# A decoder step on one core: the front of the first token group put in another order

## The chip, the cores and the metric

One core of a Trainium2 chip runs the whole program in one launch. The metric is the device time of that execution in microseconds (us), the median of several runs. Everything is computed in f32.

## What is computed

One layer of a decoder for 1024 prompt tokens and 8 x 4 sample tokens with the same weights, model width 1024:

```
n    = RMSNorm(x)
proj = n @ w_in            -> q | k | v | u, v_c (gelu) | mem q | gate logits
A    = chunk gating:  u * (tril(W_s) RMSNorm(v_c) + b), 128-token chunks
B    = sliding-window attention, 8 q heads / 2 kv heads, sinks, ALiBi
C    = cross-attention of 4 heads into 256 memory rows,
       k_m, v_m = RMSNorm(mem) @ w_mem_kv
h    = x + (sum_j sigmoid(gate_j) * (branch_j @ W_j)) @ w_out
y    = h + PEER(RMSNorm(h)): 8 heads, top 16 of 128^2 experts per head;
       per token 128 rows of peer_u, gelu of their dots, 128 rows of peer_v
out  = RMSNorm(y); caches of k, v, mem k, mem v are outputs too
```

## The kernel before

**Tiles and groups.** Tokens lie in nine tiles of 128 (the last one is the 32 sample tokens). Tiles form four groups, (0), (1, 2), (3, 4, 5), (6, 7, 8). Everything up to the expert queries is the *front* of a group. The expert part runs in *batches*: a batch gathers 4 rows of `peer_u` and 4 of `peer_v` for each of 128 tokens (0.5 MB a DMA, by index, issued by GpSimd), 32 batches to a prompt tile. Group 0's front has no batches beside it; the front of group g+1 is spread over the batches of group g.

**The order.** `front_units(g)` (L115) writes a group's front as a list of units. `build_steps` (L334) puts group 0's list, up to the experts of its first quarter of heads, ahead of all batches, and spreads the other lists with `spread_out`, by the costs of `costs` (L190) and the dependences of `waits_a_step` (L206). Each of the engines TensorE (`pe`, L900), ScalarE (`act`, L1252), VectorE (`dve`, L1480) and the DMA queue SyncE (`sp`, L709) walks the same list and does its own part of every unit, strictly in that order; semaphores tie the parts together. So a unit's place sets its place in four queues. GpSimd (L1867) has a list of its own: two selects that make the chunk matrices triangular, then all gathers.

**Units of group 0's front**, with their lines: `load_x`, `load_mem` (SP, L734 and L745); `square` (ScalarE, L1258: Square with the row's mean as its accumulator, then Sqrt) and `scale` (VectorE, L1501: the inverse root with one Newton step by `inverse_root`, L1486, then the row is scaled in place), argument 0 for x, 1 and 2 for the memory rows; `turn` (TensorE transposes through the identity, L907, L914; VectorE copies them into `xnT` times the norm's weight, L1508, L1515); `chunk` (L941, L948; ScalarE Gelu and mean square, L1290); `chunk_norm` (VectorE, L1518; for tile 0 it first waits for all constants of `second_in` and makes small tables); `block` (L917, L930: one 128-column block of the input projection; the four `u` blocks here, the eight q and memory-q blocks and k later); `spatial` (L951, L959; L1532; TensorE waits for GpSimd's two selects by `made`); `mem_k`, `mem_v`, `mem_turn` (L962 to L987); `values`; `scores` (L989; VectorE adds the bias and takes maxima, L1554, `m_ready`); `exps` (ScalarE, L1311); `divide` (L1585); `probs` (transposes, L1015); `mix` (L1032); `gate` (L1149: eight chunks of a gate block into one PSUM bank, four of the branch's projection into another; ScalarE Tanh, L1390; VectorE product and sum, L1662); `out` (L1173, L1679); `square_h`, `norm_h`, `turn_h` (L1400, L1689, L1183); `query` (L1193); `keys` and the top-k units.

**Gates.** There are 24 of a group, `("gate", g, i, j)` for 8 column blocks i and 3 branches j; `gate_order(0)` is (1, 0, 2). The first one in order needs only the chunk branch's features (`u_ready`), which are there before the softmax. VectorE's part of the first waits until the memory branch's mix is done, because `merged`, `sig` and `prod` share the buffer `area` with the scores: `sc` at 0 to 2047, `scT` at 2048 to 4095; `merged` at 0, `sig` at 3072, `prod` at 3840. Tile 0 uses only the second half of each head's keys in `sc` and `scT`.

**PSUM.** Each unit's results go to the next of six banks in turn (`SPOT`, `TURN`, L417); a writer waits for the reader of the bank's last user (`free`, `gone`).

**Weights.** They are streamed by SP into six slots of 2 MB (`LOADS`, L440; the rings of the gathers serve as four of them in group 0). A load is issued when the unit in `FREED` has read its slot. At the start SP issues x, the constants `FIRST`, weight 0 (`vc`), the ten constants `SECOND` and the attention bias, the two memory tiles, `load_hb(0)` (x again, for the residual) and the next five weights (L866 to L883).

**Tables.** ScalarE's functions need the right table; a load stands as ACT_TABLE_LOAD in the trace. Sqrt, Gelu and Exp/Tanh sit in different ones.

Of the kernel before, what the change touches and what calls it, by code (L numbers as in the profile page):

```python
# [14 lines left out]
DC = D // P  # L15
# [99 lines left out]
def front_units(g):  # L115
    tiles = GROUP_TILES[g]
    prompt = [t for t in tiles if t < PTILES]
    out = [("load_x", t) for t in tiles] + [("load_mem", m) for m in range(MT)] + [("square", 0), ("scale", 0)] if g == 0 else []
    out += [("turn", feed(t)) for t in tiles]
    out += [("chunk", t) for t in tiles] + [("chunk_norm", t) for t in tiles]  # L120
    if g == 0:
        out += [("square", 1), ("square", 2), ("scale", 1), ("scale", 2)]
    out += [("block", g, WK + 1 + n) for n in range(CG)]
    out += [("spatial", t) for t in tiles]
    if g == 0:
        out += [("turn", 1), ("turn", 2)]
        out += [("mem_k", m) for m in range(MT)] + [("mem_v", m) for m in range(MT)] + [("mem_turn", m) for m in range(MT)]
    out += [("block", g, n) for n in range(FU)]
    out += [("block", g, WK)]
    for n, t in enumerate(prompt):  # L130
        if n == 0:
            out += [("values", x) for x in tiles]
        out += [("scores", t)]
        out += [("exps", t), ("divide", t)]
        if n:
            out += [("mix", prompt[n - 1])]
        out += [("probs", t)]
    out += [("mix", prompt[-1]), ("keep_k", g)]
    if PTILES in tiles:
        out += [("smp_load", 0), ("knat", 0), ("smp_scores", 0)] + [("smp_mem", b) for b in range(0, 3)]  # L140
        out += [("smp_turn", 0)] + [("smp_mem", b) for b in range(3, 6)]
        out += [("smp_soft", 0)] + [("smp_mem", b) for b in range(6, B)]
        out += [("smp_probs", 0), ("smp_mem_turn", 0), ("smp_mem_soft", 0), ("smp_mix", 0), ("smp_mem_probs", 0)]
        out += [("smp_mem_mix", b) for b in range(B)]
        out += [("smp_mem_out", 0)]
    out += [("gate", g, i, j) for i in range(DC) for j in gate_order(i)]
    out += [("load_hb", t) for t in tiles if g or not starts_group(t)]
    out += [("out", t, half) for half in range(2) for t in tiles]
    out += [("square_h", t) for t in tiles]
    out += [("norm_h", t) for t in tiles]  # L150
    out += [("turn_h", t) for t in tiles]
    if PTILES in tiles:
        out += [("pack_root", 0)]
    out += [("query", g, n) for n in range(2 * PH)]
    return out
# [373 lines left out]
def build(nc, t):  # L529

    ctx = ExitStack()
    with ctx:
# [110 lines left out]
        def left(*name):  # L643
# [29 lines left out]
        y_stored = [sem(f"y_stored{n}") for n in range(2)]  # L673
        mem_stored, vc_stored, stored = sem("mem_stored"), sem("vc_stored"), sem("stored")

        FIRST = dict(ident=ident, norm1_col=norm1_col)
        SECOND = dict(chunk_g=chunk_g, ws_T=ws_T, ws_T_smp=ws_T_smp[0:SAMPLE], chunk_b=chunk_b, mem_norm_col=mem_norm_col,
                      gate_b=gate_b, sinks=sinks, idents=idents, iota16=iota16, smp_sinks=smp_sinks)
        CONSTS = dict(subT=subT, norm2_g=norm2_g, final_g=final_g)
        PACKED = 16 * (GROUPS - 1 + 2 * GROUPS)  # L680
# [29 lines left out]
        def _(sp):  # L710
# [155 lines left out]
            for n, units in STEPS:  # L866
                if n is not None:
                    expert(n)
                for u in units:
                    if u[0] in DO:  # L870
                        DO[u[0]](*u[1:])
                    if u == ("load_mem", 1):
                        load_hb(0)
                    if u == ("load_x", 0):
                        for name, a in FIRST.items():
                            send(a, t[name], first_in)
                        load_w(0)
                        for name, a in SECOND.items():
                            send(a, t[name], second_in)
                        send(bias[:, :], t["swa_bias"][:, 0, :], second_in)  # L880
                    if u == ("load_mem", 1):
                        for n_w in range(1, SLOTS_W):
                            load_w(n_w)  # L883
                    if u == ("mix", 0):
                        for name, a in CONSTS.items():
                            send(a, t[name], consts_in)
                    if u in FREED and w_next(FREED[u]) is not None:
# [365 lines left out]
        def _(act):  # L1253
# [3 lines left out]

            def square(n):  # L1258
                R = rows_of(n)
                act.wait_ge(x_in[XBUF[n]], 16 * x_before(n)[1])  # L1260
                A.settle()
                A.add(fn(n_dump[0:R, :], x_buf[0:R, XBUF[n], :], ACT.Square, scale=D ** -0.5, accum_out=mean_x[0:R, n:n + 1]))
                A.settle()
                A.add(fn(root_x[0:R, n:n + 1], mean_x[0:R, n:n + 1], ACT.Sqrt, bias=eps[0:R, :]), x_squared, n + 1)
# [134 lines left out]

            def square_h(x):  # L1400
                R, k = width(x), local(x) // P
                act.wait_ge(*gone("out", x, 1))
                act.wait_ge(*gone("out", x, 0))
                A.settle()
# [76 lines left out]
        def _(dve):  # L1481
# [179 lines left out]

            def gate(g, i, j):  # L1662
                k, W = NBR * i + j, tokens(g)
                if i == 0 and j == gate_order(i)[0]:
                    V.settle()
                    dve.wait_ge(f_mm, upto("mmix", max(x for x in GROUP_TILES[g] if x < PTILES)))
                dve.wait_ge(*gone("gate", g, i, j))
# [200 lines left out]
        def _(pool):  # L1868
            g = nc.gpsimd

            pool.wait_ge(second_in, 16 * (len(SECOND) + 1))
            g.affine_select(out=ws_T[:, :, :], in_=ws_T[:, :, :], compare_op=ALU.is_ge, fill=0.0, base=0,
                            pattern=[[0, CG], [1, P]], channel_multiplier=-1).then_inc(made, 1)
# [151 lines left out]
```

## Time and profile before

| | |
|---|---|
| median of 3 runs | 3387.99 us (3387.7 to 3388.31) |
| profiled execution, span from first to last instruction | 3390.4 us |
| TensorE busy / VectorE / GpSimd / ScalarE | 83% / 73% / 62% / 21% |
| DMA moved | 1317 MB, mean 388 GB/s |
| granted TensorE clock, mean | 0.92 |

For the profiled execution only its span is known; it is 2.4 us above the median of the runs. In the profile PE is TensorE's matmuls, PEld its weight loads, DVE VectorE, ACT ScalarE, POOL GpSimd, SP SyncE; SPq and POOLq are the queues of DMA issues. L948 is line 948 of the kernel. "out<-in" names the tiles of an instruction. In brackets stands the idle time of the engine before an instruction and what ended it. A matmul of the source in f32 stands as two or more rows of the hardware, so the counts (x16 for eight chunks) are higher than in the code. Ends of matmuls are modelled. The granted clock of 1.00 is 2.4 GHz, 0.50 is 1.2 GHz. Shares of DMA are those of the core's 16 DMA engines.

### The profile page before, as it was taken

How to read it: one execution, taken by the hardware profiler on the slowest of the kernel's cores; microseconds unless marked ns; L12 is line 12 of the kernel's file. 1: busy time of each engine (PE TensorE's matmuls, PEld its weight loads, DVE VectorE, ACT ScalarE, POOL GpSimd, SP SyncE). 2: the span in 40 equal slices, each digit the busy share in tenths (PEclk: the TensorE clock that was granted, in tenths of full speed). 3: DMA queues.
4: the chain of work that ended last, by engine and by line, in shares of the span. 5: the costliest groups of instructions: out<-in, count | busy, mean ns of one | idle time of the engine just before them, and what ended most of it. 6: DMA issues, size and time to landing. Idle time of an engine off the chain costs nothing.

```text
span 3390.4 us, 30958 instructions
## 1 busy us (share of the span) xinstructions
PE 2829.6 (83%) x9130; PEld 1588.7 (47%) x9130; DVE 2488.4 (73%) x5814; ACT 708.3 (21%) x1819; POOL 2109.5 (62%) x2118
## 2 busy tenths in 40 slices
PE   8979898889898988979887788878887777777777
PEld 5857585645454543534544455433443333333321
DVE  1257976789988888778887877777777767777764
ACT  2122311221321112213131111111221211221211
POOL 0034655556676666667677665567677777777775
PEclk9989999999899998989996799988998889898989
DMA  8759999999999999999999999999999999999997
GB/s 297 288 225 385 346 406 396 407 379 403 377 396 410 410 407 406 399 406 392 408 394 409 409 410 410 410 406 392 407 397 402 410 409 409 398 401 408 408 398 305
DMA packets 375158, 1317.04 MB, mean 388 GB/s; under 512 B 38592, under 2 KB 43552, under 8 KB 374976
## 3 DMA queue, kind: packets, MB, share of 16 engines
q0 software_dynamic: 304128, 1107.43, 82.9%
q1 hardware_dynamic: 70864, 207.63, 15.9%
q8 instruction: 75, 1.23, 0.1%
q14 instruction: 91, 0.75, 0.1%
HBM read 1303.64 MB, written 12.26 MB: 388 GB/s over the span
## 4 chain that ended last, share of the span: by engine, by line
POOL 26%; PE 23%; DMA 22%; issue 14%; DVE 12%; ACT 2%; SPq 0%; DVEq 0%; POOLq 0%; ACTq 0%
DMA v_ring_sb<-peer_v,i_all_sb 16%; POOL u_ring_sb L1892 13%; POOL v_ring_sb L1904 13%; PE ps L1234 9%; DVE u_ring_sb L1803 5%; PE ps L1165 4%; DMA u_ring_sb<-peer_u,i_all_sb 3%; PE ps L1201 2%; PE ps L930 2%; PE ps L1170 2%; DVE h_buf_sb L1817 2%; PE ps L1180 2%; PE ps L948 1%; DMA v_ring_sb<-peer_v,i_packed_sb 1%; ACT area_sb L1315 1%
## 5 line engine op out<-in xcount | busy, mean ns | idle before, releaser
L1234 PE MATMUL ps<-v_ring_sb,diag_sb 128*128 128x512 f32 (+1 forms) x2840 | 1452.5, 664 | 441.9 <-DMA v_ring_sb<-peer_v,i_all_sb 384.5
L1892 POOL DMA_INDIRECT u_ring_sb<-peer_u,i_all_sb x1024 | 1026.7, 1003 | 770.5 <-DVE u_ring_sb L1803 304.3
L1803 DVE SCALAR_TENSOR_TENSOR u_ring_sb<-u_ring_sb,ps 128x1024 f32<-128x1024 f32 x1056 | 1252.1, 1216 | 255.1 <-DMA u_ring_sb<-peer_u,i_all_sb 221.0
L1904 POOL DMA_INDIRECT v_ring_sb<-peer_v,i_all_sb x1024 | 1021.4, 997 | 446.5 <-issue 279.5
L1234 PEld LDWEIGHTS ps<-v_ring_sb,diag_sb 128*128 128x128 f32 (+1 forms) x2840 | 573.6, 208 | 1229.2 <-issue 680.9
L1817 DVE SCALAR_TENSOR_TENSOR h_buf_sb<-v_ring_sb,c_sb,h_buf_sb 128x1024 f32<-128x1024 f32 x346 | 444.9, 1286 | 281.4 <-DMA v_ring_sb<-peer_v,i_all_sb 258.5
L1447 ACT ACTIVATE diag_sb<-ident_sb,c_sb 128x128 f32<-128x128 f32 x678 | 226.1, 392 | 1415.7 <-DVE c_sb L1813 1410.8
L1165 PE MATMUL ps<-xnT_sb,w_ring_sb 128*128 128x256 f32 (+3 forms) x1280 | 329.4, 411 | 1.7 <-DVE feats_sb L1610 1.7
L1165 PEld LDWEIGHTS ps<-xnT_sb,w_ring_sb 128*128 128x128 f32 x1280 | 234.5, 191 | 99.6 <-issue 28.1
L1201 PE MATMUL ps<-xnT_sb,w_ring_sb 128*128 128x256 f32 (+3 forms) x896 | 220.2, 405 | 4.4 <-DMA w_ring_sb<-w_q 4.4
L1201 PEld LDWEIGHTS ps<-xnT_sb,w_ring_sb 128*128 128x128 f32 x896 | 161.2, 192 | 66.0 <-issue 10.0
L1460 ACT ACTIVATE gelu_sb<-act_sb 128x4 f32<-128x4 f32 x264 | 54.0, 205 | 651.0 <-DVE u_ring_sb L1803 650.3
L930 PE MATMUL ps<-xnT_sb,w_ring_sb 128*128 128x384 f32 (+3 forms) x704 | 178.1, 412 | 3.8 <-DMA w_ring_sb<-w_vvc 3.8
L1170 PE MATMUL ps<-feats_sb,w_ring_sb 128*128 128x256 f32 (+3 forms) x640 | 170.1, 409 | 0.0
L930 PEld LDWEIGHTS ps<-xnT_sb,w_ring_sb 128*128 128x128 f32 x704 | 129.3, 193 | 53.1 <-issue 7.2
L1170 PEld LDWEIGHTS ps<-feats_sb,w_ring_sb 128*128 128x128 f32 x640 | 117.2, 190 | 40.5
L1180 PE MATMUL ps<-w_ring_sb,area_sb 128*128 128x512 f32 (+1 forms) x256 | 119.1, 622 | 9.4 <-DMA w_ring_sb<-w_out 5.7
L1813 DVE TENSOR_TENSOR c_sb<-gelu_sb,g_all_sb 128x4 f32<-128x4 f32 x256 | 42.7, 167 | 62.4 <-ACT gelu_sb L1460 29.5
L1803 DVE DVE_READ_ACCUMULATOR u_ring_sb<-u_ring_sb,ps 128x1 f32 x1056 | 86.4, 82 | 0.0
L1180 PEld LDWEIGHTS ps<-w_ring_sb,area_sb 128*128 128x128 f32 (+1 forms) x256 | 48.6, 191 | 78.8 <-issue 72.4
L1397 ACT ACTIVATE area_sb<-ps,gate_b_sb 128x128 f32<-128x128 f32 (+3 forms) x96 | 45.6, 475 | 168.2 <-PE ps L1165 159.2
L1460 ACT ACT_TABLE_LOAD x55 | 70.6, 1283 | 1.0
(241 smaller groups left out, 2018.2 us busy)
## 6 DMA issues: line engine op xcount, KB each, us to landing
w_ring_sb<-w_d SPq DMA_DIRECT2D x40, 1536.0 KB, 10.7
w_ring_sb<-w_q SPq DMA_DIRECT2D x14, 2048.0 KB, 20.3
w_ring_sb<-w_b SPq DMA_DIRECT2D x10, 2048.0 KB, 15.4
u_ring_sb<-peer_u,i_all_sb POOLq DMA_INDIRECT x1024, 14.2
v_ring_sb<-peer_v,i_all_sb POOLq DMA_INDIRECT x1024, 14.2
w_ring_sb<-w_out SPq DMA_DIRECT2D x6, 2048.0 KB, 19.3
w_ring_sb<-w_vvc SPq DMA_DIRECT2D x4, 2048.0 KB, 15.3
feats_sb<-x SPq DMA_DIRECT2D x12, 512.0 KB, 23.5
```

The costliest lines, as they stand in the source:

```text
L930: last = mm(bank("block", g, n)[:, 0:W], w[:, c, :], xnT[:, c, 0:W], start=c == 0, stop=c == DC - 1)
L1165: last = mm(bank("gate", g, i, j)[:, 0:W], w[:, c, :], xnT[:, c, 0:W], start=c == 0, stop=c == DC - 1)
L1170: last = mm(bank("proj", g, i, j)[:, 0:W], w[:, DC + c, :], feats[:, branch + c, 0:W], start=c == 0, stop=c == BC - 1)
L1180: last = mm(bank("out", x, half)[0:R, :], merged[:, c, W], w[:, c, :], start=c == 0, stop=c == DC - 1)
L1201: last = mm(bank("query", g, n)[:, 0:W], w[:, c, n % 4 * P:(n % 4 + 1) * P], xnT[:, c, 0:W], start=c == 0, stop=c == DC - 1)
L1234: last = mm(ps[0:M, half, :], diag[:, n % 2, j, 0:M], v_ring[:, n % 2, j, half * 512:(half + 1) * 512], start=opens, stop=closes)
L1447: A.add(fn(diag[:, (n - 1) % 2, j, 0:M], (ident if M == P else idents)[:, :], ACT.Copy, scale=c4[:, (n - 1) % 2, j:j + 1]), diags, TENSOR_ ...
L1460: A.add(fn(gelu4[:, n % 2, :], act4[:, n % 2, :], ACT.Gelu), gelus, n + 1)
L1803: V.add(v.scalar_tensor_tensor(u, u, 1.0, n2_cur[:, :], ALU.mult, ALU.mult, accum_out=act4[:, n % 2, j:j + 1]), dots, NB * n + j + 1)
L1817: V.add(v.scalar_tensor_tensor(h_buf[:, x % 2, :], v_ring[:, n % 2, j, :], c4[:, n % 2, j:j + 1], h_buf[:, x % 2, :], ALU.mult, ALU.add), ...
L1892: g.indirect_dma_start(u_ring[:, n % 2, j, :], None, t["peer_u"], index(n, j)).then_inc(u_in[n % 2][j], 16)
L1904: g.indirect_dma_start(v_ring[:, n % 2, j, :], None, t["peer_v"], index(n, j)).then_inc(v_in[n % 2][j], 16)
```

## The change

1. In group 0 the memory rows' `square` and `scale` come ahead of `chunk`, and their `turn` right behind `chunk`, ahead of `chunk_norm`. They were behind `chunk_norm` and behind `spatial`.
2. The first gate, `("gate", 0, 0, 1)`, comes between `scores` and `exps` of tile 0. VectorE's wait for the memory mix moves to the second gate of group 0.
3. The ten constants of `SECOND` less `mem_norm_col`, and the bias, are issued by GpSimd ahead of its selects; `mem_norm_col` joins `FIRST` on SP. The second load of x (`load_hb(0)`) moves on SP from the start to the place of `mix` of tile 0.
4. ScalarE does a Sqrt of `eps` into the root's tile at the head of `square(0)`, before it waits for x, and at the head of `square_h` of each group's first tile, before it waits for the output projection. The true root overwrites it.

```diff
@@ -117,13 +117,15 @@
     prompt = [t for t in tiles if t < PTILES]
     out = [("load_x", t) for t in tiles] + [("load_mem", m) for m in range(MT)] + [("square", 0), ("scale", 0)] if g == 0 else []
     out += [("turn", feed(t)) for t in tiles]
-    out += [("chunk", t) for t in tiles] + [("chunk_norm", t) for t in tiles]
     if g == 0:
         out += [("square", 1), ("square", 2), ("scale", 1), ("scale", 2)]
+    out += [("chunk", t) for t in tiles]
+    if g == 0:
+        out += [("turn", 1), ("turn", 2)]
+    out += [("chunk_norm", t) for t in tiles]
     out += [("block", g, WK + 1 + n) for n in range(CG)]
     out += [("spatial", t) for t in tiles]
     if g == 0:
-        out += [("turn", 1), ("turn", 2)]
         out += [("mem_k", m) for m in range(MT)] + [("mem_v", m) for m in range(MT)] + [("mem_turn", m) for m in range(MT)]
     out += [("block", g, n) for n in range(FU)]
     out += [("block", g, WK)]
@@ -131,6 +133,8 @@
         if n == 0:
             out += [("values", x) for x in tiles]
         out += [("scores", t)]
+        if g == 0:
+            out += [("gate", 0, 0, gate_order(0)[0])]
         out += [("exps", t), ("divide", t)]
         if n:
             out += [("mix", prompt[n - 1])]
@@ -143,7 +147,7 @@
         out += [("smp_probs", 0), ("smp_mem_turn", 0), ("smp_mem_soft", 0), ("smp_mix", 0), ("smp_mem_probs", 0)]
         out += [("smp_mem_mix", b) for b in range(B)]
         out += [("smp_mem_out", 0)]
-    out += [("gate", g, i, j) for i in range(DC) for j in gate_order(i)]
+    out += [("gate", g, i, j) for i in range(DC) for j in gate_order(i)][1 if g == 0 else 0:]
     out += [("load_hb", t) for t in tiles if g or not starts_group(t)]
     out += [("out", t, half) for half in range(2) for t in tiles]
     out += [("square_h", t) for t in tiles]
@@ -673,8 +677,8 @@
         y_stored = [sem(f"y_stored{n}") for n in range(2)]
         mem_stored, vc_stored, stored = sem("mem_stored"), sem("vc_stored"), sem("stored")
 
-        FIRST = dict(ident=ident, norm1_col=norm1_col)
-        SECOND = dict(chunk_g=chunk_g, ws_T=ws_T, ws_T_smp=ws_T_smp[0:SAMPLE], chunk_b=chunk_b, mem_norm_col=mem_norm_col,
+        FIRST = dict(ident=ident, norm1_col=norm1_col, mem_norm_col=mem_norm_col)
+        SECOND = dict(chunk_g=chunk_g, ws_T=ws_T, ws_T_smp=ws_T_smp[0:SAMPLE], chunk_b=chunk_b,
                       gate_b=gate_b, sinks=sinks, idents=idents, iota16=iota16, smp_sinks=smp_sinks)
         CONSTS = dict(subT=subT, norm2_g=norm2_g, final_g=final_g)
         PACKED = 16 * (GROUPS - 1 + 2 * GROUPS)
@@ -869,19 +873,15 @@
                 for u in units:
                     if u[0] in DO:
                         DO[u[0]](*u[1:])
-                    if u == ("load_mem", 1):
-                        load_hb(0)
                     if u == ("load_x", 0):
                         for name, a in FIRST.items():
                             send(a, t[name], first_in)
                         load_w(0)
-                        for name, a in SECOND.items():
-                            send(a, t[name], second_in)
-                        send(bias[:, :], t["swa_bias"][:, 0, :], second_in)
                     if u == ("load_mem", 1):
                         for n_w in range(1, SLOTS_W):
                             load_w(n_w)
                     if u == ("mix", 0):
+                        load_hb(0)
                         for name, a in CONSTS.items():
                             send(a, t[name], consts_in)
                     if u in FREED and w_next(FREED[u]) is not None:
@@ -1257,6 +1257,8 @@
 
             def square(n):
                 R = rows_of(n)
+                if n == 0:
+                    A.add(fn(root_x[0:R, n:n + 1], eps[0:R, :], ACT.Sqrt))
                 act.wait_ge(x_in[XBUF[n]], 16 * x_before(n)[1])
                 A.settle()
                 A.add(fn(n_dump[0:R, :], x_buf[0:R, XBUF[n], :], ACT.Square, scale=D ** -0.5, accum_out=mean_x[0:R, n:n + 1]))
@@ -1399,6 +1401,8 @@
 
             def square_h(x):
                 R, k = width(x), local(x) // P
+                if starts_group(x):
+                    A.add(fn(root_h[0:R, x:x + 1], eps[0:R, :], ACT.Sqrt))
                 act.wait_ge(*gone("out", x, 1))
                 act.wait_ge(*gone("out", x, 0))
                 A.settle()
@@ -1661,7 +1665,7 @@
 
             def gate(g, i, j):
                 k, W = NBR * i + j, tokens(g)
-                if i == 0 and j == gate_order(i)[0]:
+                if i == 0 and j == gate_order(i)[1 if g == 0 else 0]:
                     V.settle()
                     dve.wait_ge(f_mm, upto("mmix", max(x for x in GROUP_TILES[g] if x < PTILES)))
                 dve.wait_ge(*gone("gate", g, i, j))
@@ -1868,6 +1872,9 @@
         def _(pool):
             g = nc.gpsimd
 
+            for name, a in SECOND.items():
+                g.dma_start(a, t[name]).then_inc(second_in, 16)
+            g.dma_start(bias[:, :], t["swa_bias"][:, 0, :]).then_inc(second_in, 16)
             pool.wait_ge(second_in, 16 * (len(SECOND) + 1))
             g.affine_select(out=ws_T[:, :, :], in_=ws_T[:, :, :], compare_op=ALU.is_ge, fill=0.0, base=0,
                             pattern=[[0, CG], [1, P]], channel_multiplier=-1).then_inc(made, 1)
```

## Rows read from the trace of the kernel before

**Rows 1.** Windows: length, busy us of PE, PEld, DVE, ACT, POOL; clock, DMA share, GB/s
```profile
0.00:215.00 215.00, 188.01 (x1241) 154.36 (x1242) 51.63 (x179) 46.42 (x114) 1.10 (x6) 0.95 0.67 246
215.00:3390.40 3175.40, 2641.58 (x7891) 1434.33 (x7890) 2436.73 (x5635) 661.92 (x1706) 2108.40 (x2112) 0.92 1.01 398
```

**Rows 2.** Chain of work that ended last, in order of time, front: start us, us, what
```profile
11.51 11.95 DMA u_ring_sb<-w_b
...
23.50 7.41 PE ps L930 x64
...
31.81 1.75 PE ps L914 x16
33.55 2.28 issue
35.83 15.67 PE ps L970 x32
51.50 13.73 PE ps L979 x32
...
102.83 1.79 PE ps L1165 x16
104.61 0.89 PE ps L1170 x8
```

**Rows 3.** Timeline, softmax of tile 0: start us, us, engine, line, operation [idle before]
```profile
88.16 0.40 ACT L1315 ACTIVATE area_sb<-area_sb,row_sb 128x128 f32<-128x128 f32 x1 [2.58 <-DVE row_sb L1577]
...
93.20 1.97 PE L1021 MATMUL ps<-ident_sb,area_sb 128*128 128x128 f32 x8 [5.66 <-DVE area_sb L1592]
...
99.98 1.95 PE L1165 MATMUL ps<-xnT_sb,u_ring_sb 128*128 128x128 f32 x16
...
101.97 0.37 ACT L1397 ACTIVATE area_sb<-ps,gate_b_sb 128x128 f32<-128x128 f32 x1 [0.99 <-PE ps L1165]
```

**Rows 4.** Timeline, behind the output projection
```profile
181.25 1.28 ACT L1407 ACT_TABLE_LOAD   x1
182.54 0.29 ACT L1407 ACTIVATE root_h_sb<-mean_h_sb,eps_sb 128x1 f32<-128x1 f32 x1
...
185.15 1.97 PE L1190 MATMUL ps<-ident_sb,area_sb 128*128 128x128 f32 x8 [5.91 <-DVE area_sb L1695]
```

**Rows 5.** Timeline, start of the front
```profile
4.50 1.28 ACT L1262 ACT_TABLE_LOAD   x1 [4.50 <-DMA feats_sb<-x]
...
13.16 9.96 PE L948 MATMUL ps<-w_ring_sb,xnT_sb 128*128 128x512 f32 x16 [0.83 <-issue]
...
25.82 0.29 ACT L1301 ACTIVATE root_c_sb<-mean_c_sb,eps_sb 128x1 f32<-128x1 f32 x1
...
26.20 1.06 ACT L1262 ACTIVATE n_dump_sb<-feats_sb 128x1024 bf16<-128x1024 f32 x1
```

**Rows 6.** DMA issues with KB and us to landing: first 60 us; last row whole span
```profile
w_ring_sb<-w_vvc SPq DMA_DIRECT2D x1, 2048.0 KB, 9.7
...
bias_sb<-swa_bias SPq DMA_DIRECT2D x1, 128.0 KB, 5.9
...
u_ring_sb<-peer_u,i_all_sb POOLq DMA_INDIRECT x1024, 14.2
```

**Rows 7.** Windows of 1 us with the granted clock (columns as in rows 1)
```profile
37.00:38.00 1.00, 1.00 (x2) 0.36 (x2) 0.00 (x0) 0.00 (x0) 0.00 (x0) 0.50 1.04 414
...
90.00:91.00 1.00, 0.00 (x0) 0.00 (x0) 0.00 (x0) 1.00 (x7) 0.00 (x0) 0.80 1.05 417
...
97.00:98.00 1.00, 1.00 (x4) 0.10 (x2) 0.60 (x1) 0.00 (x0) 0.00 (x0) 0.79 0.00 0
...
192.00:193.00 1.00, 1.00 (x7) 1.00 (x6) 0.00 (x0) 0.00 (x0) 0.00 (x0) 0.51 0.00 0
```

**Rows 8.** Timeline, GpSimd's first gathers
```profile
215.27 1.99 POOL L1892 DMA_INDIRECT u_ring_sb<-peer_u,i_all_sb  x1 [199.22 <-DVE g_all_sb L1785]
...
217.57 0.94 POOL L1892 DMA_INDIRECT u_ring_sb<-peer_u,i_all_sb  x1 [0.30 <-issue]
```

## Prediction, made before the changed kernel ran

> **What bounds the kernel now.** I read the busy time of two long stretches first, then the chain of work that ended last, then the timeline of the front, and last the windows with the granted clock. Up to 215 us the DMA engines are busy 67% of the time and TensorE 188 of 215 us; from there to the end the DMA share is 1.01 at 398 GB/s [rows 1]. So the body (mostly gathers) is bound by transfers: no edit of an engine's order helps there. The first 215 us are bound by TensorE's chain, and whatever is cut there starts the gathers earlier. The change works almost only in this front. In the chain of the front the reader is to see TensorE from 23.5 us on, with three holes: 2.28 us of issue at 33.55, the softmax, and the norm after the output projection [rows 2 to 4].
>
> **The change, part by part.** All times are of the profiled execution, whose span is 3390.4 us; the median of the runs, 3388.0, is 2.4 us (0.07%) less, and I take the differences over unchanged.
>
> A. *Start.* ScalarE loads a table at 4.50, after x has landed, and another between Square and root, as for h in rows 4, 1.28 us each and both on x's way to its scaling [rows 4, 5]. A Sqrt ahead of the wait makes both vanish from that way: the Square at 26.20 follows a Sqrt at 25.82 with no load between [rows 5], so the square root's table serves both. The chunk projection, which starts at 13.16, could so start at 10.6. But it also needs its weight, issued at 2.21 and landed 9.7 us later, at 11.9 [rows 6]. Its issue moves behind one more small DMA (the memory norm's column, 0.47 us), the two memory rows' DMAs (1.05 MB) now follow right behind it, and GpSimd's constants (1.03 MB) come from a second queue beside it instead of behind it. I take 12.6 us for the landing: 0.5 for the issue and 0.2 net for sharing. So the projection starts at 12.66 in place of 13.16: gain 0.5. Bounds: -0.7 (the 0.5 and another 1.2 for sharing) and +1.2 (landing unchanged at 11.9). Its 16 matmuls take 9.96 us, where 16 of the value projection's take 6.9 [rows 2, 5]: a cold start of 3.1 us, which I leave as it is.
>
> B. *The u weight.* The chunk projection ends at 23.12, the u weight lands at 23.46 and its blocks start at 23.50 [rows 2, 5]: 0.38 us idle. Now its issue does not stand behind eleven constants on SP and not behind h_buf's load (0.52 MB, at about 400 GB/s 1.3 us sooner), and the 1.75 us of memory transposes [rows 2] lie in front of these blocks. Needed at 12.66 + 9.96 + 1.75 = 24.4, there by 22.1 to 23.5: gain 0.4.
>
> C. *The 2.28 us hole.* Today TensorE waits after the transposes for VectorE's four copies before the memory keys. With the transposes ahead of 7.41 us of u blocks the copies lie under these. The memory rows' squares and scalings move to 13 to 18 us, where ScalarE and VectorE are idle under the chunk. The chunk norm now stands behind four copies on VectorE instead of behind nothing; the copies end 2 us behind the transposes, at 26, and the norm by 28, before the spatial product at 24.4 + 7.4 = 31.8. Gain 2.3. The transposes themselves are not saved.
>
> D. *The clock behind the hole.* The granted clock is 0.50, the 1.2 GHz level, at 37 to 38 us, after TensorE's 2.28 us of idleness [rows 7]. So the 32 matmuls of the keys take 15.67 us against 13.73 for the 32 of the values [rows 2]. Without the hole: gain 1.9; below 0 only if the clock falls without a hole, which no stretch here shows.
>
> E. *One gate in the softmax.* A gate with its projection is 1.79 + 0.89 = 2.68 us of TensorE [rows 2]; it leaves the stretch behind the softmax. It is put behind the memory scores, which end at 93.20 - 5.66 = 87.54 [rows 3], its first matmul some 0.2 us before that end; and its weight and u features are long there. But its Tanh stands ahead of the exponentials in ScalarE's queue. By the gate at 99.98, whose Tanh starts at 101.97 [rows 3], the new Tanh starts at about 89.35, lets the exponentials begin near 89.64 instead of 88.16 [rows 3], and all behind them (the divisions, the probabilities' transposes at 93.20) comes 1.5 us later. VectorE's product of the gate (0.29 us) waits until 90.4, with only the division behind it, due at 93. Tanh follows Exp without a load. Net gain 2.7 - 1.5 = 1.2. Bounds -0.5 (the Tanh waits for the projection as well and the gate runs at half clock) to 2.7. TensorE's hole shrinks from 5.7 to 4.5 us; I let the clock fall in it as now.
>
> F. *The root of h.* After the output projection the chain is Square, table load 1.28, root, then norm and transposes [rows 4]. The Sqrt ahead of the waits is covered by 14 us of output matmuls in which ScalarE idles. Gain 1.3. The same Sqrt in the three later groups costs ScalarE 0.3 us each, under transfers: 0.
>
> The Trainium skill, page "ScalarE: Activation LUTs", section "What ACT_TABLE_LOAD costs", gives about 2.66 us for a switch, a drain of 1.38 included. The rows disagree here: the load starts at 181.25 and the root at 182.54, 1.29 us later [rows 4]. By the page F would be 2.7 and the sum 9.0.
>
> h_buf's load goes from the start to SP's place at the end of the softmax and is needed only at 172 us; from 97 to 98 us the DMA engines stand idle [rows 7], which is room for its 0.5 MB: 0. The eleven constants are needed by VectorE before the chunk norm and by GpSimd's two selects before the spatial product. A gather costs GpSimd 0.94 us and 0.30 to the next, the first 1.99 [rows 8]: 11 such issues end at about 0.5 + 11 x 1.24 + 1.05 = 15.2 us. The SP queue's last constant landed 5.9 us after issue [rows 6]: 21 us. There is slack to about 28.8 us (31.8, less some 3 us of preparations, root and norm on VectorE): cost 0.
>
> **Sum:** 0.5 + 0.4 + 2.3 + 1.9 + 1.2 + 1.3 = 7.6 us. All weights of the front are requested as slots come free, so they move along, and the body, at full transfer rate, shifts as a block. 3388.0 - 7.6 = **3380.4**. The measurement can tell 0.2%, 6.8 us, from nothing: the border is 3381.2, which my sum passes by less than a microsecond.
>
> **Rivals.** (1) *The first weight comes late.* For: 1.03 MB of constants and 1.05 MB of memory rows now compete with it; all of them ahead of it would cost 2.08 MB / 400 GB/s = 5.2 us, a landing at 17.1. The chunk then starts 3.9 us late, the sum is 7.6 - 0.5 - 3.9 = 3.2: 3384.8. Against: constants already landed nearly in the order of issue. Chance 0.14.
> (2) *The body swallows part of it.* For: its share is already full and its slots and queues may fall into another order; half of 7.6 would give 3384.2, nothing 3388. Against: only one of its terms, bytes, sets it. Chance 0.12.
> (3) *The clock stays up in the shortened holes.* The softmax hole goes from 5.7 to 4.5 us, the one after the output from 5.8 to 4.6. Today the clock falls at about 90.6 and is back at 97.6, and behind the second hole it is back at 193.0 [rows 7]. Kept up, it would save half of the 4.4 us from 93.2 and half of some 7.1 busy us from 185.15: 2.2 + 3.5 more, 13.3 in all, 3374.7. Against: 3.1 us of idleness brought it down in the softmax, less before the memory keys. Chance 0.12.
> (4) *The constants come too late, and it is slower.* The constants go by GpSimd, whose DMAs land after a median 14.2 us in the body [rows 6]; from 15.2 us that is 29.4, a cost of 0.6, since the norm, the spatial product and all of TensorE's in-order queue stand behind them. Each microsecond past 28.8 costs one: break-even at 36.4, slower by 0.2% from 43.2; there the time is 3394.8. Against: the 14.2 us are a queue full of 0.5 MB gathers, here it is 1 MB in all. The Trainium skill speaks for it: page "SBUF — State Buffer", section "Who interferes with whom", says that VectorE in some of its modes keeps GpSimd from writing a DMA's descriptors. If all eleven issues took the first gather's 1.99 us [rows 8], the last would be out at 25.7, and the constants there about when they are needed. Chance 0.07.
> (5) *The Sqrts do not load ahead*, should Square bring its own table back: A and F fall away, 3382.2; the Square at 26.20 speaks against it, and I give it none of the chance.
>
> **How the numbers follow.** Forecast case 0.55, its own range 3378 to 3383, two thirds of it below 3381.2: 0.37; rival 3 adds 0.12, the mild ends of 1 and 2 some 0.05: faster 0.54. Slower 0.06 from rival 4; the same 0.40. The range takes in rival 3's time and most of 1 and 2: 3374.5 to 3386.
>
> **What would show it.** The first transposes at 7.8 us, the chunk at 12 to 13, memory transposes ahead of the u blocks, no hole before the memory keys and 13.7 us for these, GpSimd's selects by 22 us, exponentials starting 1.5 us behind the maxima, h's root with no load behind its Square, and the first gather near 207.7 instead of 215.3. Wrong would be: a wait of the spatial product for the constants, a chunk later than 13.2, or a first gather that is early while the end is not.

## The result, and the profile after

| | before | changed |
|---|---|---|
| median of 21 runs each | 3388.31 us (3384.7 to 3392.91) | 3383.35 us (3379.73 to 3390.13) |
| ratio | | 0.9986 (0.9980 to 0.9992) |
| span of the profiled execution | 3390.4 us | 3386.0 us |
| first gather issued | 215.27 us | 209.98 us |

The kernel became 5.0 us faster, 0.14%: less than the 7.6 us forecast, and inside the 0.2% that were called no change. The interval of the ratio does not reach 1.0000, so the gain is clear of the noise. Single runs scatter by 4 to 7 us around their median. Two executions of the runs below took 9767 and 11217 us and are left out of their ratios. The profiled execution took 3387.71 us, with this span:

```profile
span 3386.0 us, 30962 instructions
```

So the front is compared in the traces, and the ends by medians. The first gather comes 5.29 us sooner, the medians differ by 4.96: what the front gives arrives at the end.

The chain that ended last, in the changed kernel's front, in order of time (start, us, what), against [rows 2]:

```profile
2.68 11.28 DMA w_ring_sb<-w_vvc
...
14.00 9.83 PE ps L948 x16
23.83 1.75 PE ps L914 x16
25.58 7.15 PE ps L930 x64
32.72 0.89 PE ps L959 x8
33.62 13.74 PE ps L970 x32
47.35 13.73 PE ps L979 x32
```

The hole of 2.28 us ahead of the memory keys (L970) is gone and the keys take 13.74 us instead of 15.67. But the chunk projection (L948) is not ahead; it begins at 14.00 instead of 13.16, and a DMA stands in front of it. The timeline of the start says the same (in brackets: idle before, and what ended it):

```profile
8.31 1.94 PE L914 MATMUL ps<-ident_sb,feats_sb 128*128 128x128 f32 x8 [8.31 <-DVE feats_sb L1509]
...
11.75 0.63 POOL L1879 TENSOR_SCALAR_AFFINE_SELECT ws_T_sb<-ws_T_sb 128x512 f32<-128x512 f32 x1 [4.89 <-DMA bias_sb<-swa_bias]
...
14.00 9.83 PE L948 MATMUL ps<-w_ring_sb,xnT_sb 128*128 128x512 f32 x16 [3.75 <-DMA w_ring_sb<-w_vvc]
```

x's transposes (L914) start 2.08 us sooner than in the kernel before, and then TensorE waits 3.75 us for the weight. GpSimd's selects (POOL) run at 11.75 us: the constants are early, not late. Their DMA issues, and those of the weight and the memory rows, by KB and us to landing, against [rows 6]:

```profile
w_ring_sb<-w_vvc SPq DMA_DIRECT2D x1, 2048.0 KB, 11.3
...
feats_sb<-mem SPq DMA_DIRECT2D x2, 512.0 KB, 12.1
...
chunk_g_sb<-chunk_g POOLq DMA_DIRECT2D x1, 256.0 KB, 4.0
...
bias_sb<-swa_bias POOLq DMA_DIRECT2D x1, 128.0 KB, 5.4
```

The weight took 11.3 us where it took 9.7. All ten DMAs of GpSimd (nine constants and the bias, 0.98 MB) landed before it: the bias was issued at 6.32, 3.6 us behind the weight's issue at 2.68, and landed at 11.7, 2.2 us ahead of the weight. Next the softmax of tile 0 in the timeline, against [rows 3]:

```profile
79.76 1.71 PE L1005 MATMUL ps<-k_T_sb,feats_sb 64*128 64x128 f32 x16
...
85.21 0.37 ACT L1399 ACTIVATE area_sb<-ps,gate_b_sb 128x128 f32<-128x128 f32 x1 [5.07 <-PE ps L1165]
...
85.60 1.28 ACT L1317 ACT_TABLE_LOAD   x1
...
86.89 0.40 ACT L1317 ACTIVATE area_sb<-area_sb,row_sb 128x128 f32<-128x128 f32 x1
...
91.93 1.97 PE L1021 MATMUL ps<-ident_sb,area_sb 128*128 128x128 f32 x8 [5.86 <-DVE area_sb L1596]
...
99.56 1.95 PE L1165 MATMUL ps<-xnT_sb,u_ring_sb 128*128 128x128 f32 x16
```

The Tanh of the moved gate needs no table load, the exponentials behind it do. In the kernel before, that load (84.30, in the rows below) ran ahead of a wait, and the exponentials began at 88.16. Rows of the kernel before: first score matmul, load, second gate, first five query blocks:

```profile
83.90 1.71 PE L1005 MATMUL ps<-k_T_sb,feats_sb 64*128 64x128 f32 x16
...
84.30 1.28 ACT L1315 ACT_TABLE_LOAD   x1
...
102.66 1.95 PE L1165 MATMUL ps<-xnT_sb,u_ring_sb 128*128 128x128 f32 x16
...
187.85 11.62 PE L1201 MATMUL ps<-xnT_sb,v_ring_sb 128*128 128x128 f32 x80 [0.73 <-issue]
```

In the changed kernel TensorE's idle time ahead of the probabilities' transposes (L1021) is 5.86 us, no less than the 5.66 before. The windows there, with the clock in the third column from the end, against [rows 7]:

```profile
91.00:92.00 1.00, 0.07 (x1) 0.08 (x2) 0.87 (x1) 0.98 (x5) 0.00 (x0) 0.57 0.15 63
...
97.00:98.00 1.00, 1.00 (x4) 0.57 (x3) 0.45 (x1) 0.00 (x0) 0.00 (x0) 0.52 0.00 0
```

The clock falls in the 92nd microsecond and is at 1.2 GHz almost to 98. Last, behind the output projection, against [rows 4]:

```profile
178.16 0.29 ACT L1411 ACTIVATE root_h_sb<-mean_h_sb,eps_sb 128x1 f32<-128x1 f32 x1
...
180.77 1.97 PE L1190 MATMUL ps<-ident_sb,area_sb 128*128 128x128 f32 x8 [4.62 <-DVE area_sb L1699]
...
183.47 10.72 PE L1201 MATMUL ps<-xnT_sb,v_ring_sb 128*128 128x128 f32 x80 [0.73 <-issue]
...
209.98 1.92 POOL L1899 DMA_INDIRECT u_ring_sb<-peer_u,i_all_sb  x1 [197.34 <-DVE g_all_sb L1789]
```

The idle time ahead of h's transposes (L1190) went from 5.91 to 4.62 us. Step by step from start to first gather:

| stretch | forecast gain | measured |
|---|---|---|
| A: start of the chunk | 0.5 | 13.16 - 14.00 = -0.84 |
| the chunk itself | 0 | 9.96 - 9.83 = 0.13 |
| B, C, D: end of the chunk to first score matmul | 4.6 | (83.90 - 23.12) - (79.76 - 23.83) = 4.85 |
| E: first score matmul to second gate | 1.2 | (102.66 - 83.90) - (99.56 - 79.76) = -1.04 |
| F: hole ahead of h's transposes | 1.3 | 5.91 - 4.62 = 1.29 |
| first five query blocks | 0 | 11.62 - 10.72 = 0.90 |
| sum | 7.6 | 5.29 |

### The profile page after: what moved, and what is told of

The parts are those of the page before. It is cut to its first block, busy times and chain, and to the rows that moved or that the text cites. A ratio compares the mean times of both kernels' runs of the same rounds, so it can differ in the third digit from the quotient of the medians.

```text
span 3386.0 us, 30962 instructions
## 1 busy us (share of the span) xinstructions
PE 2830.4 (84%) x9130; PEld 1590.4 (47%) x9130; DVE 2488.0 (73%) x5814; ACT 708.4 (21%) x1823; POOL 2116.6 (63%) x2128
## 4 chain that ended last, share of the span: by engine, by line
POOL 28%; PE 25%; DMA 20%; issue 14%; DVE 12%; ACT 2%; DVEq 0%; SPq 0%; POOLq 0%; ACTq 0%
POOL u_ring_sb L1899 14%; DMA v_ring_sb<-peer_v,i_all_sb 14%; POOL v_ring_sb L1911 14%; PE ps L1234 9%; DVE u_ring_sb L1807 4%; PE ps L1165 4%; DMA u_ring_sb<-peer_u,i_all_sb 3%; PE ps L1201 3%; PE ps L1170 2%; PE ps L930 2%; DVE h_buf_sb L1821 2%; PE ps L1180 2%; PE ps L948 1%; DMA w_ring_sb<-w_vvc 1%; DMA v_ring_sb<-peer_v,i_packed_sb 1%
## 5 line engine op out<-in xcount | busy, mean ns | idle before, releaser
L948 PE MATMUL ps<-w_ring_sb,xnT_sb 128*128 128x512 f32 (+1 forms) x144 | 68.9, 635 | 6.2 <-DMA w_ring_sb<-w_vvc 3.7
```

The source lines that it names most:

```text
L948: last = mm(bank("chunk", x)[0:R, :], xnT[:, c, W], w[:, c, :], start=c == 0, stop=c == DC - 1)
```

## The experiments

All are the changed kernel with the edit shown, timed beside the kernel before (ratios are to that, with their 95% interval). Each interval reaches about 0.1% (3 us) or more to each side, so the medians alone cannot rank versions that lie a microsecond or two apart; the stretches of the traces, one execution each, are read for that. The question was which parts lost the time of A and E.

**The table of the exponentials, ahead.**

```diff
 def gate(g, i, j):                      # ScalarE
     k, W = NBR * i + j, tokens(g)
+    if (g, i, j) == (0, 0, 1):
+        A.add(fn(root_h[:, 0:1], eps[:, :], ACT.Exp))
     act.wait_ge(f_mm, upto("gate", g, i, j))
```

> The changed kernel with one more ScalarE instruction, an Exp of eps ahead of the wait of the first gate's Tanh. In the changed kernel the exponentials' table load (1.28 us) follows the Tanh at 85.60 and stands ahead of the exponentials at 86.89. Theory A (the load is on the path, and it is what turned the moved gate from a gain into a loss): no load between Tanh and exponentials, these begin 85.5 to 85.7, the probabilities' transposes 90.6 to 90.7, the first gather at 208.7 (1.3 us ahead of 209.98), the median 6 us under the kernel before. Rival B (the Tanh's delay alone did it, the load overlaps): first gather stays at 209.7 to 210.3.

Ratio 0.9981 (0.9972 to 0.9990), first gather at 208.10. Its softmax in the timeline:

```profile
79.91 1.28 ACT L1395 ACT_TABLE_LOAD   x1
...
84.97 0.37 ACT L1401 ACTIVATE area_sb<-ps,gate_b_sb 128x128 f32<-128x128 f32 x1 [3.56 <-PE ps L1165]
...
85.23 0.39 ACT L1317 ACTIVATE area_sb<-area_sb,row_sb 128x128 f32<-128x128 f32 x1
...
90.25 1.93 PE L1021 MATMUL ps<-ident_sb,area_sb 128*128 128x128 f32 x8 [4.43 <-DVE area_sb L1598]
...
96.71 1.95 PE L1165 MATMUL ps<-xnT_sb,u_ring_sb 128*128 128x128 f32 x16
```

The load runs at 79.91, the exponentials follow the Tanh directly, 5.72 us behind the first score matmul (79.51); 7.13 in the changed kernel, 4.26 in the kernel before. The delay by the Tanh alone is thus 1.46 us, what was forecast. From the first score matmul to the second gate it is 17.20 us, against 19.80 changed and 18.76 before: with its table ahead the gate gains 1.56 us. Of the 2.60 us between the two kernels 1.43 lie ahead of the probabilities' transposes (the load, 1.28, and the gap around it) and 1.17 behind them. These are the clock: it is at 0.50 from about 90.3 to 93.7 us here, and from 91.1 to 98.0 in the changed kernel. Theory A holds. The first gather came 1.88 us sooner and not 1.3: the 2.60 and a shorter chunk (9.27 us) less a later start (0.32) and slower query blocks:

```profile
180.61 11.69 PE L1201 MATMUL ps<-xnT_sb,v_ring_sb 128*128 128x128 f32 x80 [0.73 <-issue]
```

They took 10.72 us in the changed kernel, behind a hole of the same 4.62 us.

**The gate back behind the softmax.**

```diff
-        if g == 0:
-            out += [("gate", 0, 0, gate_order(0)[0])]
-    ... for j in gate_order(i)][1 if g == 0 else 0:]
+    ... for j in gate_order(i)]
-    if i == 0 and j == gate_order(i)[1 if g == 0 else 0]:
+    if i == 0 and j == gate_order(i)[0]:
```

> The changed kernel with the gate put back behind the softmax. Theory A (the gate inside the softmax costs more than it saves): exponentials at 88.16 less the 4.14 us that the chain is ahead, 84.0, the first gather at about 208.9, one us ahead of the changed kernel's 209.98. Rival B (the gate saves 1.2 us as forecast, and something else lost the time): first gather at 211.2.

Ratio 0.9983 (0.9974 to 0.9992), first gather at 207.46, better than either theory said. The stretch in question is as in the kernel before: exponentials 4.26 us behind the first score matmul (78.41 to 82.67), and to the second gate it is 18.75 us, 1.05 less than in the changed kernel. The rest of the 2.5 us came from the chunk, which took 8.52 us here instead of 9.83 at the same start. Its single matmuls take 1.06 us at first and 0.59 later, as those of the memory keys do at a granted clock of 0.50 and 1.00. The clock column reads 1.00 over the whole chunk, though, so only the durations show the half pace. How long it lasts differs from one execution to the next. So A holds by the stretch, and the first gather alone is no measure finer than a microsecond. The ends of this version and the one with the Exp ahead cannot be told apart by their medians.

**The constants only after the first weight.**

```diff
 def _(pool):
+    pool.wait_ge(w_in[w_slot(0)], 16)
     for name, a in SECOND.items():
         g.dma_start(a, t[name]).then_inc(second_in, 16)
```

> The changed kernel; GpSimd waits until the first weight has landed before it issues the constants. Theory A (the 1.0 MB of constants beside it delayed the first weight): it lands at about 12 instead of 13.96, the chunk starts 1.5 to 2 us sooner, the selects are at about 22, before the spatial product, and the first gather comes at 208.2. Rival B (the memory rows and the next weights behind it in the same queue delayed it): the chunk still starts at 13.7 to 14.2, the first gather at 210.

Ratio 0.9979 (0.9970 to 0.9988), first gather at 207.50. In the timeline of its start:

```profile
11.54 9.81 PE L948 MATMUL ps<-w_ring_sb,xnT_sb 128*128 128x512 f32 x16 [1.96 <-DMA w_ring_sb<-w_vvc]
...
23.50 0.63 POOL L1880 TENSOR_SCALAR_AFFINE_SELECT ws_T_sb<-ws_T_sb 128x512 f32<-128x512 f32 x1 [5.68 <-DMA bias_sb<-swa_bias]
```

The chunk starts at 11.54, 2.46 us sooner than in the changed kernel, with the memory rows and the next weight still behind the weight in its queue. The first gather moves by the same 2.48 us. The selects at 23.50 still lie ahead of the spatial product at 30.08. Theory A holds: the constants beside the weight delayed it, not what follows in its own queue.

**The constants back on SP**, between the first weight and the memory rows.

```diff
                     load_w(0)
+                    for name, a in SECOND.items():
+                        send(a, t[name], second_in)
+                    send(bias[:, :], t["swa_bias"][:, 0, :], second_in)
...
-            for name, a in SECOND.items():
-                g.dma_start(a, t[name]).then_inc(second_in, 16)
-            g.dma_start(bias[:, :], t["swa_bias"][:, 0, :]).then_inc(second_in, 16)
```

> The changed kernel with the ten constants and the bias issued by SP again, between the first weight and the memory rows as before, all else as changed. Theory A (the second queue is what delays the first weight; in the same queue the constants stand behind it): the weight lands at about 12.4 and the chunk starts there, 1.5 us or more ahead of the changed kernel's 14.0; the memory rows land by 17 and the u weight by 24.2, so nothing else is lost, first gather at 208 to 208.8, that is, GpSimd's issuing was a loss of 1.2 to 2 us. Rival B (taking the eleven issues off SP was a gain): chunk no earlier than 13.7, or the transposes of the memory rows or the u blocks wait, first gather at 209.8 or later.

Ratio 0.9982 (0.9973 to 0.9992), first gather at 207.35.

```profile
11.60 9.69 PE L951 MATMUL ps<-w_ring_sb,xnT_sb 128*128 128x512 f32 x16 [1.91 <-DMA w_ring_sb<-w_vvc]
```

The chunk starts at 11.60. Neither the transposes of the memory rows nor the u blocks wait. So the issue by GpSimd, as the change has it, was a loss of 2.4 us in the front, and the constants' place in SP's queue costs nothing. Over all profiles: with the constants on GpSimd from the start the chunk begins at 13.96, 14.00, 14.32, 14.74 and 16.64 us; with the constants late or on SP at 11.54, 11.58, 11.60 and 11.68.

The Trainium skill, page "DMA: Bandwidth & Descriptors", section "Queues, rings and completion order", says that each DMA engine takes its queue rows in turn, a packet at a time. The traces agree: the same 1 MB delays the weight from another queue (11.3 us to landing) and not from behind it in its own (8.9 us, against 8.8 when it is issued only after the landing). In the kernel before, also with the constants behind it in its own queue, the weight took 9.7 us. Two things changed at once between the queues, and no run separates them: on GpSimd's queue the first constants (0.54 MB, issued at 1.34 to 2.62) also went out ahead of the weight. An estimate at 400 GB/s gives 1.3 us for these and another 1.1 us for the 0.44 MB that were issued behind the weight's issue and still landed before it, together the 2.4 us.

**The order of the memory rows put back.**

```diff
-    if g == 0:
-        out += [("square", 1), ("square", 2), ("scale", 1), ("scale", 2)]
-    out += [("chunk", t) for t in tiles]
-    if g == 0:
-        out += [("turn", 1), ("turn", 2)]
-    out += [("chunk_norm", t) for t in tiles]
+    out += [("chunk", t) for t in tiles] + [("chunk_norm", t) for t in tiles]
+    if g == 0:
+        out += [("square", 1), ("square", 2), ("scale", 1), ("scale", 2)]
...
+        out += [("turn", 1), ("turn", 2)]
         out += [("mem_k", m) ...
```

> The changed kernel with the memory rows' squares, scalings and transposes put back behind the chunk norm and the spatial product. Theory A (the reorder is what won the front its time): the hole of 2.28 us ahead of the memory keys and their half-speed start (1.9 us) return, the keys end 4 us later, first gather at about 214, and the time is within 1 us of the kernel before. Rival B (the hole would have closed by the earlier load of the memory rows): first gather before 212.

Ratio 0.9996 (0.9986 to 1.0005), first gather at 216.66. Two rows, of the start and of the memory keys:

```profile
16.64 10.04 PE L946 MATMUL ps<-w_ring_sb,xnT_sb 128*128 128x512 f32 x16 [6.42 <-DMA w_ring_sb<-w_vvc]
```

```profile
38.78 15.67 PE L968 MATMUL ps<-u_ring_sb,xnT_sb 128*128 128x512 f32 x32 [2.31 <-issue]
```

The hole (2.31 us) and the slow keys (15.67) are back. From the start of the chunk to the first score matmul it is 86.85 - 16.64 = 70.2 us, against 65.8 in the changed kernel. Of these 4.4 us 0.2 are the chunk itself, so the reorder is worth 4.2: 2.31 of the hole and 1.93 of the keys. The gather is later than forecast, since this execution's first weight came at 16.6. That execution was also the slowest of the version's 11 (3394.04 us); the median, 3387.32, lies 2.2 us under the kernel before, whose interval takes in both no change and the 1 us of theory A.

**No Sqrt ahead**, neither in `square(0)` nor in `square_h`.

```diff
-                if n == 0:
-                    A.add(fn(root_x[0:R, n:n + 1], eps[0:R, :], ACT.Sqrt))
...
-                if starts_group(x):
-                    A.add(fn(root_h[0:R, x:x + 1], eps[0:R, :], ACT.Sqrt))
```

> The changed kernel without the Sqrt ahead of square(0) and without those ahead of square_h. Theory A (at the start it gave nothing, since the chunk waits for its weight; behind the output projection it gave its 1.28 us): x's transposes at about 10.9 instead of 8.31, the chunk still at the landing of its weight (13.9 to 16.6 in the runs so far), and TensorE's idle time ahead of h's transposes back from 4.62 to 5.9 us; first gather some 1.3 us later than in the changed kernel, for the same start of the chunk. Rival B (both gave 1.3 to 2.6 us): the chunk starts later than its weight lands, by over 0.5 us.

Ratio 0.9990 (0.9981 to 1.0000), first gather at 212.33.

```profile
10.43 1.94 PE L914 MATMUL ps<-ident_sb,feats_sb 128*128 128x128 f32 x8 [10.43 <-DVE feats_sb L1505]
...
14.74 9.43 PE L948 MATMUL ps<-w_ring_sb,xnT_sb 128*128 128x512 f32 x16 [2.37 <-DMA w_ring_sb<-w_vvc]
```

```profile
182.20 1.97 PE L1190 MATMUL ps<-ident_sb,area_sb 128*128 128x128 f32 x8 [5.90 <-DVE area_sb L1695]
```

x's transposes are 2.1 us later and the chunk still waits for its weight, 2.37 us long: at the start the Sqrt gives nothing in the changed kernel. It would matter with the constants late: there the chunk starts at 11.54, and without the Sqrt x's transposes would end at about 12.4 (10.43 + 1.94), an estimate that no run tests. Ahead of h's transposes the hole is 5.90 us again. Theory A holds; the other 1 us of the gather is the weight's later landing (0.74) and slower query blocks (11.63 us, 0.91), less 0.6 in the chunk and the softmax.

**Both mends together** (the edits of the first and the third experiment; e8 in the text below).

> The changed kernel with both mends: the Exp ahead of the moved gate's Tanh, and the constants issued only when the first weight has landed. If the two losses are separate, their gains add: chunk at 11.5, exponentials 1.28 us sooner behind the scores, second gate 17.2 us behind the start of the scores (19.8 in the changed kernel), first gather at 205 to 206, median 8 to 9 us under the kernel before and 3 to 4 under the changed one. Rival: the earlier front does not reach the end beyond what the single mends gave (about 6 to 7 us under the kernel before).

Ratio 0.9975 (0.9965 to 0.9985), median 3378.91, first gather at 205.78: 9.5 us ahead of the kernel before. The median is 9.0 us under that of the kernel before beside it. In the front the gains add: the chunk starts at 11.58, and from the first score matmul to the second gate it is 17.23 us. That they arrive at the end fits the median, but the interval (5 to 12 us) does not exclude the rival's 6 to 7.

**TensorE kept busy in its holes**, on top of both mends. The products' result is read by nobody, and the outputs are computed as before.

```diff
+            def stay_busy(count):
+                for _ in range(count):
+                    mm(ps[:, 0, 0:P], ident[:, :], ident[:, :], start=True, stop=True)
 # TensorE: turn(0):   stay_busy(6)  ahead of its wait
 #          chunk(0):  stay_busy(5)  ahead of its wait
 #          probs(0):  stay_busy(18) ahead of its wait
 #          turn_h(0): stay_busy(18) ahead of its wait
```

> e8 with products of the identity by itself, whose result nobody reads, in TensorE's idle stretches: 6 ahead of x's transposes, 5 ahead of the chunk, 18 ahead of the probabilities' transposes of tile 0, 18 ahead of h's transposes of tile 0. Theory C (what the holes cost beyond their length is the clock at 1.2 GHz behind them): the granted clock stays at 1.00 through both, the four transposes-and-mix steps behind the softmax take about 5 us instead of 7, the first five query blocks 9 us instead of 10.7 to 11.7, the chunk 7 to 9 us but then waits for the u weight until about 21.3; first gather at 200.5 to 202.5. Rival D (the products come in the way, or the clock falls anyway): first gather not before 205.

Ratio 0.9958 (0.9944 to 0.9972), median 3372.27, 15.6 us under the kernel before; first gather at 200.60, 14.7 ahead. The windows of the version without these products (length; busy us of PE, PEld, DVE, ACT, POOL; clock, DMA share, GB/s), and its first query blocks in the timeline:

```profile
88.00:90.00 2.00, 2.00 (x11) 1.70 (x10) 1.28 (x2) 1.10 (x2) 0.00 (x0) 0.53 0.55 235
...
180.00:182.00 2.00, 2.00 (x12) 2.00 (x11) 0.00 (x0) 0.03 (x1) 0.00 (x0) 0.50 0.00 0
```

```profile
178.18 11.80 PE L1201 MATMUL ps<-xnT_sb,v_ring_sb 128*128 128x128 f32 x80 [0.73 <-issue]
```

The same windows of the version with them, then its timeline:

```profile
88.00:90.00 2.00, 1.51 (x11) 1.06 (x12) 1.18 (x3) 0.69 (x2) 0.00 (x0) 1.00 0.61 258
...
180.00:182.00 2.00, 2.00 (x21) 2.00 (x20) 0.00 (x0) 0.28 (x1) 0.00 (x0) 1.00 0.00 0
```

```profile
11.68 7.13 PE L956 MATMUL ps<-w_ring_sb,xnT_sb 128*128 128x512 f32 x16
...
21.72 2.50 PE L936 MATMUL ps<-xnT_sb,u_ring_sb 128*128 128x128 f32 x20 [1.16 <-DMA u_ring_sb<-w_b]
```

```profile
168.97 4.18 PE L921 MATMUL ps<-ident_sb 128*128 128x128 f32 x36
...
173.76 1.09 PE L1202 MATMUL ps<-ident_sb,area_sb 128*128 128x128 f32 x8 [0.61 <-DVE area_sb L1713]
...
175.63 9.17 PE L1213 MATMUL ps<-xnT_sb,v_ring_sb 128*128 128x128 f32 x80 [0.79 <-issue]
...
200.60 1.92 POOL L1914 DMA_INDIRECT u_ring_sb<-peer_u,i_all_sb  x1 [176.19 <-DVE g_all_sb L1803]
```

The clock stays at 1.00, the 2.4 GHz level, in both stretches (0.53 and 0.50 without the products). The first five query blocks take 9.17 us instead of 11.80. Behind the softmax, from the first transposes to the second gate, it is 92.55 - 86.91 = 5.64 us instead of 94.27 - 87.78 = 6.49. The chunk takes 7.13 instead of 9.53, but TensorE then waits 1.16 us for the u weight. Theory C holds. The products (L921) of the two later holes end 0.41 and 0.61 us before the work that they bridge to is released, so they delay nothing. Those at the start push x's transposes from 7.65 to 8.15 us, ahead of a weight that comes later anyway. Of the 5.18 us between the two versions' first gathers the chunk gives 2.40, of which 1.4 are lost again up to the first score matmul, mostly in the wait for the u weight; behind the softmax it is 0.85, behind h's norm 3.47. The last one is large because the version without them had the slowest query blocks of all, 11.80 us; five other executions with the same hole took 10.54 to 10.72, and one 11.69. The Trainium skill, page "TensorE: Matmul & The Clock Gate", section "HAM oscillation — how this bites in real kernels", gives it as a rule that TensorE should have no long idle gaps. The traces agree: 1.00 with the gaps filled, 0.50 behind them without.

The ends follow the fronts, over all versions (the first gather is of one execution each, the ratio of all its runs):

| version | first gather, against 215.27 | ratio |
|---|---|---|
| order of the memory rows back | +1.4 | 0.9996 |
| no Sqrt ahead | -2.9 | 0.9990 |
| changed | -5.3 | 0.9986 |
| Exp ahead | -7.2 | 0.9981 |
| gate back | -7.8 | 0.9983 |
| constants late | -7.8 | 0.9979 |
| constants on SP | -7.9 | 0.9982 |
| both mends | -9.5 | 0.9975 |
| both, and kept busy | -14.7 | 0.9958 |

Behind the first gather the ten profiled executions took 3167.6 to 3176.1 us, in no clear order with their fronts; a loss of a few microseconds in the body would not be seen in one execution.

## Why the prediction was right or wrong

**The frame held.** A front bound by TensorE's chain and a body bound by transfers: what the front gave reached the end about one for one, in medians, but for the version with the memory rows' order put back, whose profiled execution was its slowest. Rival 2 (the body swallows half or all of it) fell. The time lies in the range, but the sum, 7.6 us, was 2.6 too high. Of the prediction's outcomes, faster had the chance 0.54 and the same 0.40; the same came. In the front A missed by 1.34 and E by 2.24 us, and without the 0.90 of the query blocks, which was luck (below), only 4.4 of the 7.6 would have come.

**B, C and D were right:** 4.85 measured for 4.6. The reversal gives back 2.31 for C (forecast 2.3) and 1.93 for D (1.9); the other 0.6 is B with a little of the u blocks (0.4). **F was right,** 1.29 for 1.3, and 1.28 came back when the Sqrt was taken out. The prediction's other figure for F, 2.7, did not come.

**A failed, at the step that let the first weight land at 12.6.** The price for sharing was 0.2 net; it was 1.4 more (landing at 13.96), and up to 4 in single executions, beyond the bound of -0.7. A chunk later than 13.2 was named as a sign of being wrong, and it came. It was rival 1 in kind, at a smaller price. I had costed GpSimd's issues as eleven, at the gathers' pace, 1.24 us each [rows 8]. They are ten (`mem_norm_col` stays on SP), of 0.98 MB and not 1.03, and plain copies took 0.52 to 0.73, so all were under way by 6.9 us, into the weight's own time. The late landing came from these alone; the memory rows cost nothing.

**E failed, at the sentence that Tanh follows Exp without a load.** That is true and was the wrong pair: in the new order the Tanh comes first, finds itself in the table that Gelu had left, and the Exp's load moves from ahead of a wait to behind the Tanh. It put 1.28 us on the path. The delay by the Tanh itself, 1.46 to 1.59, was as forecast (1.5). The load also kept TensorE's hole at 5.86 us instead of 4.5, and from the transposes to the next gate it took 0.85 longer than before, at half clock. So the term was 2.68 - 2.87 - 0.85 = -1.04 instead of 1.2.

**The first query blocks** gained 0.90 that was not in the sum, and that was luck. In the changed kernel the clock was at 0.50 from about 179.9 to 186.7 us. With the Exp ahead, behind a hole of the same 4.62 us, it was at 0.50 from 175.7 to 185.9, and the blocks took 11.69 us, as long as in the kernel before (11.62, behind 5.91 us). So the shorter hole does not explain the gain. Rival 3 was wrong for the change, since the clock fell in both holes as before. Kept up by other work, the clock gave 0.85 us behind the softmax, where rival 3 had 2.2, and 3.5 behind h's norm as it had (2.63 in the query blocks, 0.84 between transposes and first block), the latter against the slowest query blocks of all.

**Rival 4** (constants too late) was far off: the selects ran at 11.75 us, and even with the constants issued late they began at 23.50, 6.6 us ahead of the spatial product. The danger of the second queue was that it is too early.

Open is why the first weight landed at 16.6 in one execution and at 14.0 to 14.7 in the others of the same start, and what sets the length of the half-speed part of the chunk (8.52 to 10.04 us for the chunk in all without extra products) and of the query blocks (10.54 to 11.80).

## What to carry to other kernels

When an activation is moved ahead of another, look at which table is loaded at that point, and load the next one by hand ahead of a wait. A transfer that the start waits for should have the DMA engines for itself: put what is needed later behind it in its own queue, not into a second one. Where TensorE must wait for a few microseconds in a chain, cheap products that nobody reads can keep its clock up; here they were worth about as much as the whole change (5.18 us of the front against 5.29). And before a gain is put down to an edit, look whether other executions with the same edit have it.

## What was not expected of the hardware

GpSimd issued its ten plain copies in 0.52 to 0.73 us each, against 0.94 for an indexed one plus 0.30 between two. Tanh runs from the table that Gelu uses (no load ahead of it at 85.21), and not only from that of Exp. And 1 MB on a second queue, half of it issued first, cost a 2 MB transfer 2.4 us and more at the start (11.3 us to landing), while the same MB behind it in its own queue cost it nothing (8.9 against 8.8).
